# A transformer block pair on one core: the first loads in halves, VectorE's first steps reordered, and eleven products of ones ahead of the first projection

## What is computed

```python
def rmsnorm(x, g):
    xf = x.astype(jnp.float32)
    y = xf * lax.rsqrt(jnp.mean(xf * xf, axis=-1, keepdims=True) + EPS)
    return (y * g.astype(jnp.float32)).astype(x.dtype)

def mixer(h, w_in, conv_a, gate_up_fwd, gate_bias_fwd, gate_up_bwd, gate_bias_bwd,
          gla_head_norm, w_out):
    p = h @ w_in
    gb, gc, gv, q, k, v, go, lr_f, lr_b = split_cols(p)
    ...

def first_block(x, norm_mix_pre, ...):
    h = rmsnorm(x, norm_mix_pre[l])
    y = mixer(h, w_in[l], ...)
    x = x + rmsnorm(y, norm_mix_post[l])
    h = rmsnorm(x, norm_ffn_pre[l])
    y = conv_mlp(h, w_up[l], conv_ffn[l], w_down[l])
    x = x + rmsnorm(y, norm_ffn_post[l])
    return x
```

## Time and profile before

| | |
|---|---|
| median of three runs | 1728.67 us |
| runs | 1728.17, 1728.67, 1729.39 us |
| the profiled execution | 1729.34 us, with a span of 1727.5 us |
| PE busy | 1705.1 us, 99% of the span |
| DVE, ACT, POOL busy | 72%, 47%, 21% |
| chain that ended last | PE 90%, DVE 5%, ACT 2% |
| transfers | 190.99 MB, mean 111 GB/s |

### The profile page before, as it was taken

How to read it: one execution, slowest core, us unless ns; L and a number is a source line. 1 busy time by engine, 2 the same in 40 slices (tenths; PEclk the granted TensorE clock), 3 DMA queues, 4 the chain that set the end, 5 groups by cost and what they waited for, 6 DMA issues and landing times.

```text
span 1727.5 us, 21399 instructions
## 1 busy us (share of the span) xinstructions
PE 1705.1 (99%) x8156; PEld 1402.5 (81%) x8156; DVE 1251.5 (72%) x1603; ACT 808.3 (47%) x1090; POOL 355.5 (21%) x155
## 2 busy tenths in 40 slices
PE   7999999999999999999999999999999999999998
PEld 5888888878888788888888888877888888888787
DVE  6564677858899889999887679946476767676534
ACT  5332322245335555555554456423366566666522
POOL 3366565264100000000000000221321211211051
PEclk9999999999999999999999999999999999999999
DMA  5333222135411236555576334412311111102232
GB/s 186 110 110 110 86 86 85 35 119 171 139 64 60 86 107 209 202 177 192 176 257 217 110 109 168 163 55 73 110 43 37 37 38 36 49 22 76 80 134 98
DMA packets 72957, 190.99 MB, mean 111 GB/s; under 512 B 8992, under 2 KB 11424, under 8 KB 72864
## 3 DMA queue, kind: packets, MB, share of 16 engines
q1 hardware_dynamic: 53568, 138.76, 24.5%
q10 hardware_dynamic: 19296, 50.97, 7.9%
HBM read 139.89 MB, written 49.81 MB: 110 GB/s over the span
## 4 chain that ended last, share of the span: by engine, by line
PE 90%; DVE 5%; ACT 2%; issue 1%; DMA 1%; ACTq 0%; DVEq 0%
PE psum L871 21%; PE psum L1175 17%; PE psum L1206 9%; PE psum L910 7%; PE psum L1316 7%; PE psum L1343 5%; PE psum L1063 5%; PE psum L1243 4%; PE psum L1352 4%; PE psum L1332 3%; PE psum L892 1%; PE psum L1268 1%; PE psum L1452 1%; PE psum L924 1%; PE psum L1009 1%
## 5 line engine op out<-in xcount | busy, mean ns | idle before, releaser
L782 POOL TENSOR_TENSOR wl<-wstage,wh 128x1024 fp32r<-128x1024 f32 x64 | 165.4, 2585 | 792.3 <-ACT wh L1479 763.1
L777 POOL TENSOR_TENSOR wh<-wstage,ones 128x1024 fp32r<-128x1024 f32 x43 | 103.1, 2398 | 458.1 <-PE psum L1316 295.6
L871 PE MATMUL psum<-hh,wh 128*128 128x512 f32 x544 | 172.7, 399 | 0.0
L871 PE MATMUL psum<-hl,wh 128*128 128x512 f32 x544 | 167.8, 390 | 0.0
L871 PE MATMUL psum<-hh,wl 128*128 128x512 f32 x544 | 167.6, 389 | 0.0
L2403 DVE SCALAR_TENSOR_TENSOR cc<-uu,col,cc 128x1023 f32<-128x1023 f32 x88 | 113.0, 1284 | 16.8 <-ACT cc L1699 15.2
L2738 DVE TENSOR_TENSOR ptl<-psum,pth 128x512 fp32r<-128x512 f32 x128 | 82.5, 686 | 57.0 <-ACT pth L2006 56.9
L871 PEld LDWEIGHTS psum<-hh,wh 128*128 128x128 f32 x544 | 100.2, 188 | 24.8 <-issue 2.9
L871 PEld LDWEIGHTS psum<-hl,wh 128*128 128x128 f32 x544 | 102.1, 188 | 21.6
L871 PEld LDWEIGHTS psum<-hh,wl 128*128 128x128 f32 x544 | 102.1, 188 | 21.6
L2006 ACT ACTIVATE pth<-psum 128x1024 fp32r<-128x1024 f32 x64 | 65.3, 1021 | 80.4 <-PE psum L1332 80.4
(11 more groups left out here) (428 smaller groups left out, 4440.6 us busy)
## 6 DMA issues: line engine op xcount, KB each, us to landing
wstage<-w_units SPq DMA_DIRECT2D x116, 512.0 KB, 3.6
acts<-cc ACTq DMA_DIRECT2D x22, 512.0 KB, 2.6
yo<-w_units SPq DMA_DIRECT2D x22, 512.0 KB, 7.2
down_sums<-yo SPq DMA_DIRECT2D x22, 512.0 KB, 8.7
wstage<-down_sums SPq DMA_DIRECT2D x44, 256.0 KB, 2.7
wstage<-w_units SPq DMA_DIRECT2D x35, 256.0 KB, 2.9
mix<-spill ACTq DMA_DIRECT2D x12, 512.0 KB, 2.6
kq<-mix SPq DMA_DIRECT2D x16, 256.0 KB, 3.9
```

The source lines that it names most:

```text
L777: pool.tensor_tensor(high, stage(u), ones[:, :].unsqueeze(1).to_broadcast([P, 8, P]), ALU.mult).then_inc(w_high, 1)
L782: pool.tensor_tensor(low, stage(u), high.bitcast(F32), ALU.subtract).then_inc(w_split, 1)
L871: mm = pe.matmul(out[:, t], w[:, wslot, b, :], x[part][:, xk, t], start=start and n == 0, stop=stop and n == 2)
```

## The change

**Loads.** SyncE's queue now begins with blocks 0 to 3 of unit 1 (256 KB), the second half of tile 0 and tiles 1 to 3, then blocks 4 to 7 of unit 1, those of unit 2 in two pieces, and tiles 4 to 7. ScalarE's queue has `col`, the first half of tile 0 and blocks 0 to 3 of unit 2.

**ScalarE and VectorE.** ScalarE rounds unit 1's first blocks, tile 0 in two halves and unit 2's first blocks, then the tiles; each square stands one tile later than before, and the units' second blocks follow tile 3. VectorE takes the low parts in the same pieces, and each tile's low part stands ahead of the sum for the tile before it.

**TensorE.** `first_units` goes by tile, unit and half, and in each makes the three part products, so that the first half of tile 0 is enough to begin. Ahead of it stand eleven products of 512 columns of ones into bank 0, which is written anew later. Their operand `warm` is made by GpSimd as ones times ones, ahead of its mask.

**Semaphores.** New signals use semaphores that have other uses later (`rope_in`, `out_done`, `g_in[1]`, `yb_last`, `mask_set`, `pad_set`, `halves_done`), so later waits on these count one to three higher; those hunks are left out below.

```diff
@@ -182,6 +182,7 @@
+        _n, warm = over(("pad20", [P, 8, T], F32), ("warm", [P, 4, P], F32R))
...
@@ -517,6 +518,9 @@
+        blocks_in, other_blocks_in, half_in = rope_in, out_done, g_in[1]
+        blocks_high, blocks_low, half_high, half_low = yb_last, mask_set, pad_set, halves_done
+
...
@@ -574,9 +578,17 @@
                     sync.wait_ge(w_split, reuse)
                 sync.dma_start(wstage[:, s], w_units[dram_unit(u)]).then_inc(w_loaded[s], DMA)
 
-            load(1, 1, None)
-            for b in range(0, KT, 4):
-                sync.dma_start(wstage[:, 0, b:b + 4], w_units[dram_unit(2)][:, b:b + 4]).then_inc(w_loaded[0], DMA)
+            def first_blocks(u, blocks, signal):
+
+                sync.dma_start(wstage[:, u % STG, blocks], w_units[dram_unit(u)][:, blocks]).then_inc(signal, DMA)
+
+            first_blocks(1, slice(0, 4), blocks_in)
+            sync.dma_start(xin[:, 0, T1], xT[0][:, T1]).then_inc(half_in, DMA)
+            for k in range(1, 4):
+                sync.dma_start(xin[:, k, :], xT[k]).then_inc(tile_in[k], DMA)
+            first_blocks(1, slice(4, 8), w_loaded[1])
+            for b in (4, 6):
+                first_blocks(2, slice(b, b + 2), w_loaded[0])
             for k in range(4, KT):
                 sync.dma_start(xin[:, k, :], xT[k]).then_inc(tile_in[k], DMA)
             sync.dma_start(rks[:, :, :], w_units[0][:, :, 0:32]).then_inc(rank_in, DMA)
@@ -758,6 +770,9 @@
             pool.memset(ones[:, :], 1.0)
             pool.memset(epsc[:, 1:2], EPS * CH)
             pool.memset(epsc[:, 0:1], EPS).then_inc(ones_set, 1)
+            pool.wait_ge(ones_set, 1)
+            each = ones[:, :].unsqueeze(1).to_broadcast([P, 4, P])
+            pool.tensor_tensor(warm[:, :, :], each, each, ALU.mult).then_inc(ones_set, 1)
 
             pool.memset(m01[:, :], 1.0).then_inc(m01_set, 1)
             pool.wait_ge(m01_set, 1)
@@ -879,18 +894,24 @@
 
             def first_units():
 
+                def step(u, k, half):
+
+                    t = slice(half * HT, half * HT + HT)
+                    for n, (w, x) in enumerate(((wh, hh), (wl, hh), (wh, hl))):
+                        if (u, n) == (1, 2):
+                            pe.wait_ge(*((half_low, 1) if k == half == 0 else (h_lo, k + 1)))
+                        mm = pe.matmul(slot(u)[:, t], w[:, u, k, :], x[:, k, t], start=k == n == 0,
+                                       stop=k == KT - 1 and n == 2)
+                    return mm
+
                 for k in range(KT):
-                    pe.wait_ge(h_hi, k + 1)
                     for u in (1, 2):
-                        if k == 0:
-                            pe.wait_ge(w_split, u)
-                        for n, (w, x) in enumerate(((wh, hh), (wl, hh), (wh, hl))):
-                            if (u, n) == (1, 2):
-                                pe.wait_ge(h_lo, k + 1)
-                            for half in range(2):
-                                t = slice(half * HT, half * HT + HT)
-                                mm = pe.matmul(slot(u)[:, t], w[:, u, k, :], x[:, k, t], start=k == n == 0,
-                                               stop=k == KT - 1 and n == 2)
+                        if k in (0, 4):
+                            pe.wait_ge(w_split if k else blocks_low, u)
+                        for half in range(2):
+                            if u == 1:
+                                pe.wait_ge(*((half_high, 1) if k == half == 0 else (h_hi, k + 1)))
+                            mm = step(u, k, half)
                         if k == KT - 1:
                             mm.then_inc(unit_done, 1)
 
@@ -932,7 +953,14 @@
 
 
             H = (hh, hl)
-            pe.wait_ge(ones_set, 1)
+            def warm_up():
+
+                one, wide = warm[:, 0, :], warm[:, :, :]
+                for _n in range(11):
+                    pe.matmul(bank(0), one, wide, start=True, stop=True)
+
+            pe.wait_ge(ones_set, 2)
+            warm_up()
             first_units()
             pe.wait_ge(w_split, 3)
             ranks(0)
@@ -1460,17 +1488,28 @@
         def _(act):
 
             act.dma_start(col[:, :], cols).then_inc(col_in, DMA)
-            for k in range(4):
-                act.dma_start(xin[:, k, :], xT[k]).then_inc(tile_in[k], DMA)
-
-            def high_and_square(src, gain, k, t, used, meanwhile=None):
-
-                act.activation(hh[:, k, t], src, ACT.Copy, scale=col[:, gain + k:gain + k + 1]).then_inc(h_hi, 1)
-                if meanwhile is not None:
-                    weight_high(meanwhile)
+            act.dma_start(xin[:, 0, T0], xT[0][:, T0]).then_inc(tile_in[0], DMA)
+            act.dma_start(wstage[:, 0, 0:4], w_units[dram_unit(2)][:, 0:4]).then_inc(other_blocks_in, DMA)
+
+            def high(src, gain, k, t, signal):
+                act.activation(hh[:, k, t], src, ACT.Copy, scale=col[:, gain + k:gain + k + 1]).then_inc(signal, 1)
+
+            def square(src, k, t, used):
                 if k >= 3:
                     act.wait_ge(sq_used, used + k - 2)
                 act.activation(sq[:, k % 2, t] if k else root[:, t], src, ACT.Square).then_inc(sq_ready, 1)
+
+            def high_and_square(src, gain, k, t, used):
+                high(src, gain, k, t, h_hi)
+                square(src, k, t, used)
+
+            def first_high(u, loaded):
+                act.wait_ge(loaded, DMA)
+                act.activation(wh[:, u, 0:4], wstage[:, u % STG, 0:4], ACT.Copy).then_inc(blocks_high, 1)
+
+            def other_high(u):
+                act.wait_ge(*staged(u))
+                act.activation(wh[:, u, 4:8], wstage[:, u % STG, 4:8], ACT.Copy).then_inc(w_act, 1)
 
             def weight_high(u, signal=None, by=1):
                 act.wait_ge(*staged(u))
@@ -1485,11 +1524,21 @@
                 act.wait_ge(half_sum, count)
                 take_root(root[:, half * HT:half * HT + HT], bank(n), D, 0, half_root)
 
-            weight_high(1)
+            first_high(1, blocks_in)
             act.wait_ge(col_in, DMA)
-            for k in range(KT):
+            act.wait_ge(tile_in[0], DMA)
+            high(xin[:, 0, T0], C_PRE, 0, T0, half_high)
+            act.wait_ge(half_in, DMA)
+            high(xin[:, 0, T1], C_PRE, 0, T1, h_hi)
+            first_high(2, other_blocks_in)
+            for k in range(1, KT):
                 act.wait_ge(tile_in[k], DMA)
-                high_and_square(xin[:, k, :], C_PRE, k, slice(0, T), 0, None if k else 2)
+                high(xin[:, k, :], C_PRE, k, slice(0, T), h_hi)
+                if k == 3:
+                    other_high(1)
+                    other_high(2)
+                square(xin[:, k - 1, :], k - 1, slice(0, T), 0)
+            square(xin[:, KT - 1, :], KT - 1, slice(0, T), 0)
             weight_high(3)
             act.wait_ge(norm_sum, 1)
             act.wait_ge(ones_set, 1)
...
@@ -2149,23 +2198,35 @@
                 dve.tensor_tensor(rkw[:, :, :], rks[:, :, :], col[:, C_PRE:C_PRE + KT].unsqueeze(2).to_broadcast([P, KT, 32]),
                                   ALU.mult).then_inc(w_split, 1)
 
-            first_low(1)
-            for k in range(KT):
-                low_of(xin[:, k, :], C_PRE, k, slice(0, T), k + 1)
-                if k == 0:
-                    first_low(2)
+            def blocks_of(u, blocks, high_done, signal):
+                dve.wait_ge(*high_done)
+                dve.tensor_tensor(wl[:, u, blocks], wstage[:, u % STG, blocks], f32(wh[:, u, blocks]),
+                                  ALU.subtract).then_inc(signal, 1)
+
+            blocks_of(1, slice(0, 4), (blocks_high, 1), blocks_low)
+            dve.wait_ge(half_high, 1)
+            dve.scalar_tensor_tensor(hl[:, 0, T0], xin[:, 0, T0], col[:, C_PRE:C_PRE + 1], f32(hh[:, 0, T0]),
+                                     ALU.mult, ALU.subtract).then_inc(half_low, 1)
+            low_of(xin[:, 0, T1], C_PRE, 0, T1, 1)
+            blocks_of(2, slice(0, 4), (blocks_high, 2), blocks_low)
+            low_of(xin[:, 1, :], C_PRE, 1, slice(0, T), 2)
+            for k in range(1, KT):
+                if k + 1 < KT:
+                    low_of(xin[:, k + 1, :], C_PRE, k + 1, slice(0, T), k + 2)
+                if k == 2:
+                    blocks_of(1, slice(4, 8), (w_act, 1), w_split)
+                    blocks_of(2, slice(4, 8), (w_act, 2), w_split)
                 if k == 5:
                     first_ranks()
-                if k:
-                    dve.wait_ge(sq_ready, k + 1)
-                    dve.tensor_tensor(root[:, :], root[:, :], sq[:, k % 2, :], ALU.add).then_inc(sq_used, 1)
-                    dve.wait_ge(sq_used, k)
+                dve.wait_ge(sq_ready, k + 1)
+                dve.tensor_tensor(root[:, :], root[:, :], sq[:, k % 2, :], ALU.add).then_inc(sq_used, 1)
+                dve.wait_ge(sq_used, k)
 
             dve.wait_ge(const_in, 3 * DMA)
             for n in range(4):
                 dve.tensor_copy(mask[:, :, n * P:(n + 1) * P],
```

(18 more changed lines are left out.)

2 lines of the change are left out of this document (1 added, 1 removed).

## The result

| kernel | median, us | runs | profiled execution, us |
|---|---|---|---|
| before | 1728.45 (1727.79 to 1729.39) | 6 | 1729.34 |
| changed | 1734.59 (1733.88 to 1736.24) | 6 | 1733.88 |

The ratio is 1.0036, with a 95% interval of 1.0026 to 1.0047: slower by 6.1 us. Forecast were 2.8 us less than the 1728.67 known then, and the time lies outside the range.

The account below looks back on a forecast made before the run. It took the opening to bound the kernel: TensorE's 8.7 us wait for tile 0 and its slow clock. First units ending at 29.94 instead of 32.74 gave 2.8 us less, 1725.9 us; range 1724.6 to 1727.3.

Parts of the forecast that it names:

- Part 1: Opening on TensorE: eleven products of ones run from 2.36 to 7.04 us, moving the slow-clock stretch ahead of true products.
- Part 2: Loads in halves: first true product near 7.0, unit 2's blocks landing at 8.0, unit 2 starting at 9.5.
- limit 2: End of TensorE's first units if unit 2 starts at 9.5 and 90 products follow: 29.94 us.
- Rival B: GpSimd holds `warm` back, delaying the ones: 1724.9 plus the hold once over 1.0 us; chance 0.05.
- Rival C: The ones do not wake TensorE's clock, so the slow stretch falls on true products: 1726.9 us; chance 0.06.
- A: Unit 2's blocks land in time, near 7, so first units end at 28.9: 1724.9 us; chance 0.20.
- D: Low parts come late at tile 4 or the start; 1 us past the cover gives 1726.9; chance 0.06.
- the first step: TensorE's waits: its only large one is the first, 8.7 us, so time won at the start reaches the end.
- Part 3: Low parts ahead of sums on VectorE: ready for tile 4 with 0.4 us to spare; later sum and reciprocal cost nothing.
- The cover: The squares' sum ends near 29, and is read only after the first half's rank products, near 31.8.
- Rival E: What is won is given back at a later wait: 1728.7 us; chance 0.03.

Follow-up runs that it names:

- first run: The changed kernel with GpSimd splitting no unit until VectorE's four mask casts are done: 1726.23 us, ratio 0.9987.
- casts moved: The changed kernel with the mask's source in its own buffer and the four casts behind the first gate's bias, GpSimd not held: 1726.28 us, ratio 0.9986.
- the four added operations: The kernel before with four more 1024-column GpSimd operations behind unit 3's split, into spare memory: 1729.81 us, ratio 1.0009.

## Why the prediction was wrong

**Right: the start.** Part 1 (ones from 2.19, full pace at the first true product, no hold of GpSimd), Part 2 (unit 2's blocks landing at 8.05 for 8.0, its start and its idle) and limit 2 (30.10 for 29.94) hold within 0.2 us. Rival B fell: `warm` took 1.04 us from 1.09 on, the ones began at 2.19, and nothing like the 5.95 us of the Trainium skill's "GPSIMD Engine Reference", section 2.1 "Instruction dispatch", is seen. Rival C fell, and A and D did not arise. With GpSimd out of the way the kernel takes 1726.2, against 1725.9 forecast. The range is right for that kernel.

**Wrong: the first step.** "What is won there reaches the end, because every later step is released by TensorE or by something released by it." VectorE's last sum and its casts are not: they stand at the end of VectorE's own work, which runs almost without a gap from 11.77 (before from 11.60), so the sum could start at 28.03 where it had started at 27.89. GpSimd's split of unit 4 does follow TensorE. The change moved one of two chains by 3.3 us and not the other, and the operations of both hold each other up.

**Wrong: Part 3's costs of nothing.** "The squares' sum, a step later now, ends near 29", "The reciprocal at 38.51 follows TensorE's sums and shifts with them" and "All that costs nothing". The root did shift, to 35.1, but the reciprocal stood at 38.72: it waited for the casts, and for them the prediction had no term. Alone the last sum would have ended at 28.03 + 1.22 = 29.25. The slack behind it was 35.1 (the root) less 29.25 less 0.9 of casts, 4.95 us. The sum's meeting took 2.1 and the casts' 6.4 (7.32 less 0.90), 8.5 together, 3.55 too much, and the reciprocal was 3.6 us late. The cover was named (the rank products) but not measured against what shares it: I costed VectorE's operations at their durations alone. No rival named this path, and all of slower by over 0.2% had a chance of 0.05. The signs stood in rows that I had quoted. GpSimd's 3.25 us at 28.11 against a median of 2.40 was explained away as no mark of a first call, and not asked what it was a mark of. The same line's maximum of 3.27 said that it recurs. And the casts of before, of which one took 2.38 us and the others 0.28, were not looked at. The Trainium skill, "GPSIMD Engine Reference", section 8 "Key points", names this contention, and I did not weigh it.

**Rival E** (the won time given back at a later wait) was the right kind with a chance of 0.03, and too cheap: it was priced at no gain, 1728.7. A wait that forms late can exceed what was won, by the second meeting that it causes (2.6 to 6.4 us) and the clock behind it. Against it stood "no wait of TensorE over 1.3 us", which tells only that a wait is not there yet, not how near it is. The slack of the gate's chain is what to read, and it was small: before, `lrl` ended at 49.18 and its product stood at 50.05, so 0.9 us of delay in the reciprocal were covered. It came 3.6 late, which makes 2.7, near the 2.6 us of wait with the split of unit 6 held.

## What to carry to other kernels

When an edit moves one engine's chain against another's, list for every pair of engines that can block each other which of their operations will newly lie side by side, and take an operation's unusually long record (3.25 for 2.40) as the sign of such a pair. An engine that never waits can still be near to it: measure the slack of each consumer that will come sooner, before crediting a gain at the start to the end. Where a small gain depends on such timing, pin the order with a semaphore: one wait on GpSimd turned 6.1 us of loss into 2.1 of gain.

## What was not expected of the hardware

- In these runs VectorE and GpSimd excluded each other by whole instructions, both ways: a cast of 256 columns (0.28 us) took up to 2.5, a sum of 1.22 took 3.30, and GpSimd's 2.40 became 3.2. Not all of VectorE's work is held: the reciprocal took 6.55 us with GpSimd at work during 2.3 us of it (changed kernel) or nearly all of it (first run), and the scalings that read PSUM took 1.22 both beside GpSimd and without it.
- After 4.8 us of products of ones, an idle of 1.84 us was followed by a slow stretch (0.50 from 9.9 to 13.2), while one of 1.26 us behind the ones (casts moved) and a wait of 2.6 us in the steady state were not. What makes the difference is not shown.
- A multiply of 1024 columns on GpSimd with the same tile as both inputs took 1.94 us (the four added operations), with two tiles 2.40.
- The runs of one kernel (without ones, GpSimd free) fell into two kinds, 8 us apart. In the profiled one of the short kind TensorE ended the first units 0.7 us later than in the changed kernel; that this decides is inferred.
